# One-run operand for the up products, halved first block and last tile, spins, and bias rows spread in the first MLP

## The reference

```python
def first_block(x, ...):
    h = x
    for layer in range(DEPTH):              # 0: gated linear attention, 1: window attention
        h = h + mixer(rmsnorm(h, ln_mix[layer]))
        h = h + sq_relu_mlp(rmsnorm(h, ln_mlp[layer]), w_up[layer], w_down[layer])
    return rmsnorm(h, ln_final)

def second_block(x, p, ...):
    x = x + (gate_a * y_a + gate_b * y_b) @ w_out      # full and dilated attention
    x = x + jnp.square(jax.nn.relu(rmsnorm(x) @ w_ff1)) @ w_ff2
    gate_p = jax.nn.sigmoid(rmsnorm(x) @ w_ple_gate)
    x = x + gate_p * (p @ w_ple)
    return rmsnorm(x, final_norm_g)
```

## Time and profile before

| | us |
|---|---|
| median of 3 runs | 1064.34 (1063.89 to 1066.04) |
| the profiled execution | 1064.24 |
| its span, first to last instruction | 1062.4 |
| TensorE busy | 1012.1 |
| VectorE busy | 676.2 |
| ScalarE busy | 489.3 |
| GpSimd busy | 42.8 |

### The profile page before, as it was taken

The page is one execution under the profiler, slowest core; times in us unless marked ns, Lnnn a source line. Parts: engine busy times, 40 slices in busy tenths (PEclk is TensorE's granted clock), DMA queues, the critical chain, the costliest instruction groups (busy, mean ns, idle before and its releaser), DMA issues.

```text
span 1062.4 us, 12980 instructions
## 1 busy us (share of the span) xinstructions
PE 1012.1 (95%) x5384; PEld 849.5 (80%) x5384; DVE 676.2 (64%) x945; ACT 489.3 (46%) x573; POOL 42.8 (4%) x57
## 2 busy tenths in 40 slices
PE   6989999999999889999999999899999999999996
PEld 5866778888888767888888889877877788888875
DVE  4665766566656885754666656676656675466664
ACT  4353445344445653544444454334563454344452
POOL 1000100000000000000000013300000000000000
PEclk9989999999999999999999999999999999999999
DMA  7772376545564314765455555632335656545451
GB/s 214 249 262 80 119 238 224 173 160 197 199 214 143 120 50 149 250 217 197 159 188 180 201 183 161 196 100 80 99 109 178 195 175 215 188 159 197 180 175 43
DMA packets 115027, 180.99 MB, mean 170 GB/s; under 512 B 4351, under 2 KB 78567, under 8 KB 114968
## 3 DMA queue, kind: packets, MB, share of 16 engines
q1 hardware_dynamic: 114968, 180.16, 50.8%
HBM read 179.05 MB, written 5.55 MB: 174 GB/s over the span
## 4 chain that ended last, share of the span: by engine, by line
PE 85%; DVE 7%; ACT 2%; DMA 2%; POOL 2%; issue 1%; SPq 0%; DVEq 0%; POOLq 0%; ACTq 0%
PE ps L265 82%; PE ps L269 3%; DMA raw<-in_a_w_in 2%; DVE wlo L941 2%; DVE M L949 1%; DVE M L941 1%; POOL st L2186 1%; ACT M L1692 1%; ACT RR L1695 1%; ACT whi L1695 1%; POOL M L2186 0%; DVE M L945 0%; ACT M L1695 0%; DMA x<-in_x 0%; POOL st L2183 0%
## 5 line engine op out<-in xcount | busy, mean ns | idle before, releaser
L265 PE MATMUL ps<-whi,RR 128*128 128x512 f32 (+2 forms) x1568 | 494.6, 390 | 9.7 <-DVE wlo L941 6.0
L1695 ACT ACTIVATE whi<-raw 128x2048 fp32r<-128x2048 f32 (+1 forms) x161 | 302.3, 1881 | 196.6 <-PE ps L265 179.9
L941 DVE TENSOR_TENSOR wlo<-raw,whi 128x1024 fp32r<-128x1024 f32 (+1 forms) x322 | 372.5, 1200 | 29.9 <-ACT whi L1695 29.7
L265 PE MATMUL ps<-RR,whi 128*128 128x512 f32 (+1 forms) x1248 | 362.8, 357 | 10.9 <-DVE RR L949 5.6
L265 PEld LDWEIGHTS ps<-whi,RR 128*128 128x128 f32 x1568 | 293.9, 189 | 74.8 <-issue 9.6
L265 PE MATMUL ps<-wlo,RR 128*128 128x512 f32 (+2 forms) x784 | 303.2, 387 | 0.0
L265 PE MATMUL ps<-RR,wlo 128*128 128x256 f32 (+1 forms) x1008 | 284.5, 282 | 0.0
L265 PEld LDWEIGHTS ps<-RR,whi 128*128 128x128 f32 x1248 | 220.3, 190 | 50.6 <-issue 8.3
L265 PEld LDWEIGHTS ps<-RR,wlo 128*128 128x128 f32 (+1 forms) x1008 | 191.5, 190 | 0.9
L265 PEld LDWEIGHTS ps<-wlo,RR 128*128 128x128 f32 x784 | 148.4, 189 | 27.7
L941 DVE TENSOR_TENSOR M<-M,ps 128x512 f32<-128x512 f32 x56 | 38.5, 687 | 181.7 <-ACT M L1695 173.8
(11 more groups left out here) (88 smaller groups left out, 381.7 us busy)
## 6 DMA issues: line engine op xcount, KB each, us to landing
raw<-in_w_up SPq DMA_DIRECT2D x32, 1024.0 KB, 5.4
raw<-in_w_down SPq DMA_DIRECT2D x32, 1024.0 KB, 5.0
raw<-in_w_ff SPq DMA_DIRECT2D x32, 1024.0 KB, 5.3
raw<-in_w_in SPq DMA_DIRECT2D x23, 1024.0 KB, 5.1
raw<-in_a_w_in SPq DMA_DIRECT2D x12, 1024.0 KB, 7.1
raw<-in_a_w_out SPq DMA_DIRECT2D x4, 1024.0 KB, 5.0
raw<-in_b_w_q SPq DMA_DIRECT2D x4, 1024.0 KB, 5.3
raw<-in_b_w_out SPq DMA_DIRECT2D x4, 1024.0 KB, 5.0
```

The lines of the kernel that those rows point to most:

```text
L265: return pe.matmul(out, lhsT, rhs, start=start, stop=stop, skip_group_check=True)
L941: return dve.tensor_tensor(out, a, b, op)
L1695: return act.activation(out, in_, ACT.Copy, **k)
```

## The change

- `hT` and `hT2`: the high and the low part of a group k now lie side by side, so the up product's moving operand is one run of 512 columns, and the halves that others use are its two halves.
- Start: POOL writes the ones first. TensorE multiplies the ones by themselves, 128 columns, four times ahead of the gain's transpose and five times after it, into an unused bank. x and block 0 are loaded by halves in turn (x columns 0 to 511, rows 0 to 511 of the block, and the others). ACT and DVE split the first four groups of x, the first half of block 0, the other four groups, the second half. TensorE's first product goes by halves: groups 0 to 3 for both of its parts, then 4 to 7. The scale row (`rows_scale(0)`) comes after the second block instead of the first, and DVE evacuates both blocks then.
- The spreads of the bias rows: four DMAs each, one behind each of the loads up to block 18 (toe1) to 21 and 22 (toe2) to 25, and the bias of the first attention is read after block 29 instead of 20.
- End: the last product's last tile goes in two halves of 256 columns. The square is scaled inside ACT; POOL adds the sums one by one and takes the power. The gain is multiplied in before the power is known, into `SG`, and the last factor is left: ACT does it for rows 0 to 127, DVE for the others. The stores read `SG`.

```diff
@@ Views @@
-        self.hT, self.yT = parts(0), parts(4096)
-
-        self.hT2 = RR[:, 0:4096].rearrange("p (a k t) -> p k a t", a=2, t=T)
+        self.hT2 = RR[:, 0:4096].rearrange("p (k n) -> p k n", k=8)
+        self.hT, self.yT = (self.hT2[:, :, 0:T], self.hT2[:, :, T:2 * T]), parts(4096)
...
+LAST = [(0, 0, 512), (1, 0, 512), (0, 512, 1024), (1, 512, 768), (1, 768, 1024)]
@@ tensor_program: gemm_a, gemm_up, start, last product @@
-            for w_ in due(K.at("w_lo", j)):
-                pe.wait_ge(*w_)
...
-                        for w_ in due(ready(k)):
+                        for w_ in due(K.at("w_lo", (0, 0) if j == 0 and k < 4 else j), ready(k)):
...
-                        mm(b[:, i, :].rearrange("p (a t) -> p a t", a=2), hi[:, k, 128 * i:128 * i + 128],
-                           V.hT2[:, k, :, :], k == 0, False)
+                        mm(b[:, i, :], hi[:, k, 128 * i:128 * i + 128], V.hT2[:, k, :], k == 0, False)
...
+    def spin(n):
+
+        for w in due(K.at("ones")):
+            pe.wait_ge(*w)
+        for _ in range(n):
+            mm(K.banks[:, 3, 0:128], V.S["ones"][:, :], V.S["ones"][:, :], True, True)
+
+    spin(4)
     tile = ("g", 0)
...
     tr(b[:, 0:16], V.M[0:16, 0:128]).then_inc(*K.filled(tile))
+    spin(5)
     norm_rest(0)
...
-        if f == 0:
+        if f == 256:
             rows_scale(0)
...
-    g = gemm_a(("qk",), W, 0, 1024, hT, h_ready(0), None, after_qk)
+    g = gemm_a(("qk",), W, 0, 1024, hT, h_ready(0), lambda: None, after_qk)
...
-    run_all((gemm_b(("pg",), A["w_ple_gate_2"][0], 0, D, hT, h_ready(6)), 1))
+    ready = h_ready(6)
+    for f in (0, 512):
+        bs = acc_pair()
+        tiles = [(("pg", i), take(("pg", i), misc() if i == 4 else bs[LAST[i][0]])) + LAST[i]
+                 for i in range(5) if LAST[i][1] // 512 * 512 == f]
+        for k0 in (0, 4):
+            j, hi, lo = block(A["w_ple_gate_2"][0][k0 * 128:k0 * 128 + 512, f:f + 512], 4, 512)
+            for tile, b, c, n0, n1 in tiles:
+                for k in range(k0, k0 + 4):
...
+                    t = prod(b[:, 0:n1 - n0], hT[0][:, k, c * 128:c * 128 + 128], hT[1][:, k, c * 128:c * 128 + 128],
+                             hi[:, k - k0, n0 - f:n1 - f], lo[:, k - k0, n0 - f:n1 - f], k == 0, k == 7)
...
@@ vector_program @@
-    norm_rest(0)
-    lows_to(1)
+    def first_low(i):
+
+        h = slice(1024 * i, 1024 * i + 1024)
+        for w in due(K.at("w_hi", (0, 0) if i == 0 else 0)):
+            dve.wait_ge(*w)
+        tt(V.lo[:, 0, h], V.raw[:, 0, h], V.hi[:, 0, h].bitcast(F32), ALU.subtract).then_inc(
+            *K.up("w_lo", (0, 0) if i == 0 else 0))
+
+    norm_early(0)
+    first_low(0)
+    norm_turn(0, 2)
+    norm_turn(0, 3)
+    first_low(1)
+    block["lo"] = 1
     squares(0, *all_x(K, 0))
...
         if f == 0:
             diagonals(0)
+        if f == 256:
             rows_scale(0)
...
+        for f2 in {0: [], 256: [0, 256]}.get(f, [f]):
...
+    def gain(i):
+        c, n0, n1 = LAST[i]
+        for w in due(K.at("x_end", i), K.dma("fin")):
+            dve.wait_ge(*w)
+        tt(V.SG[:, c, n0:n1], x[:, c, n0:n1], M[:, n0:n1], ALU.mult).then_inc(*K.up("x_gain", i))
+
+    take()
+    take()
+    add(0)
+    add(1)
+    take()
+    gain(0)
+    gain(1)
+    take()
+    for i in (2, 3, 4):
+        add(i)
+    for i in (2, 3, 4):
+        gain(i)
+    for n in range(2):
+        s = V.SG[:, 1, 512 * n:512 * n + 512]
+        for w in due(K.at("rstd", ("end", 1)), K.at("x_gain", 4)):
+            dve.wait_ge(*w)
+        ts(s, s, st[:, 49:50], None, ALU.mult, None).then_inc(*K.up("y_end", (1, n)))
@@ scalar_program @@
-    norm_rest(0)
-    highs_to(1)
...
+    norm_early(0)
+    first_high(0)
+    norm_turn(0, 2)
+    norm_turn(0, 3)
+    first_high(1)
+    block["hi"] = 1
...
+        actf(V.PW[:, c, n0:n1], x[:, c, n0:n1], ACT.Square, scale=1.0 / 32, accum_out=st[:, 40 + i:41 + i]).then_inc(
+            *K.up("end_sq", i))
...
+    take()
+    take()
+    sig(2)
+    sig(3)
+    square(2)
+    sig(4)
+    square(3)
+    square(4)
+    for n in range(2):
+        s = V.SG[:, 0, 512 * n:512 * n + 512]
+        for w in due(K.at("rstd", ("end", 0)), K.at("x_gain", 2)):
+            act.wait_ge(*w)
+        copy(s, s, scale=st[:, 48:49]).then_inc(*K.up("y_first", (0, n)))
@@ pool_program @@
+    memset("ones", S["ones"][:, :], 1.0)
     memset("tab_end", S["tab"][32:33, :], -1e30)
     memset("half", S["half_"][:, :], -0.5)
-    memset("ones", S["ones"][:, :], 1.0)
...
@@ sync_program @@
         load("x%d" % n, 0, V.x[:, :, n * 512:n * 512 + 512], xd[:, :, n * 512:n * 512 + 512])
+        w = K.blocks[0][0][512 * n:512 * n + 512, :] if K.blocks else A["a_w_in"][0][0:512, 0:256]
+        load("w0" if n else "w_first", 0, V.raw[:, 0, 1024 * n:1024 * n + 1024].rearrange("p (k n) -> p k n", k=4),
+             w.rearrange("(k p) n -> p k n", p=128))
+    state["block"] = 1
     weights_to(4)
...
-    load("toe1", 0, A["toe1"], bass.AP(tensor=A["scr1"].tensor, offset=127, ap=[[383, 16], [-1, 128], [1, 256]]),
-         K.dma("scr1"))
-    load("toe2", 0, A["toe2"], bass.AP(tensor=A["scr2"].tensor, offset=127, ap=[[511, 12], [-1, 128], [1, 384]]),
-         K.dma("scr2", 2))
     weights_to(9)
...
-    weights_to(21)
-    load("bias", 0, V.BS, A["toe1"].rearrange("h p c -> p h c"), K.dma("toe1"), K.full(("to", 1, 1)))
+    for i in range(4):
+        weights_to(19 + i)
+        load("toe1", i, A["toe1"][4 * i:4 * i + 4], bass.AP(tensor=A["scr1"].tensor, offset=127 + 383 * 4 * i, ap=[
+            [383, 4], [-1, 128], [1, 256]]), K.dma("scr1"))
+    for i in range(4):
+        weights_to(23 + i)
+        load("toe2", i, A["toe2"][3 * i:3 * i + 3], bass.AP(tensor=A["scr2"].tensor, offset=127 + 511 * 3 * i, ap=[
+            [511, 3], [-1, 128], [1, 384]]), K.dma("scr2", 2))
+    weights_to(30)
+    load("bias", 0, V.BS, A["toe1"].rearrange("h p c -> p h c"), K.dma("toe1", 3), K.full(("to", 1, 1)))
...
-                 V.x[:, c, n * 512:n * 512 + 512], K.at("y_end", (c, n)))
+                 V.SG[:, c, n * 512:n * 512 + 512], K.at("y_end" if c else "y_first", (c, n)))
```

More of the change, by code:

```diff
@@ L925, in tensor_program @@
     run_all((g, 1))
-    run_all((gemm_b(("pg",), A["w_ple_gate_2"][0], 0, D, hT, h_ready(6)), 1))
+    ready = h_ready(6)
[7 more added lines that the diff above has]
+                for k in range(k0, k0 + 4):
+                    for w in due(K.at("w_lo", j), ready(k)):
+                        pe.wait_ge(*w)
+                    t = prod(b[:, 0:n1 - n0], hT[0][:, k, c * 128:c * 128 + 128], hT[1][:, k, c * 128:c * 128 + 128],
+                             hi[:, k - k0, n0 - f:n1 - f], lo[:, k - k0, n0 - f:n1 - f], k == 0, k == 7)
+                if k0:
+                    t.then_inc(*K.filled(tile))
+            if k0:
+                K.value["w_used", j] = K.full(tile)
+            else:
+                t.then_inc(*K.up("w_used", j))
 def vector_program(dve, K, V):
@@ L1153, in ev_qk @@
     def ev_qk(f):
-        tile = ("qk", f)
         if f == 0:
             diagonals(0)
+        if f == 256:
             rows_scale(0)
[L1158 to L1161, removed]
+        for f2 in {0: [], 256: [0, 256]}.get(f, [f]):
+            tile = ("qk", f2)
+            for w in due(K.full(tile), *rb(0)):
+                dve.wait_ge(*w)
+            stt(M[:, 2 * f2:2 * f2 + 512], K.bank(tile), 128 ** -0.5 if f2 < 512 else 1.0, RB[:, :], ALU.mult,
+                ALU.mult).then_inc(*K.emptied(tile))
         count["qk"] += 1
@@ L1669, in vector_program, with add @@
     run_all((g, 1))
-    run_all((gemm_b(1024, 8, ev_pg), 1))
-    for c in range(2):
-        for w in due(K.at("rstd", ("end", c)), K.dma("fin")):
+    def add(i):
+        c, n0, n1 = LAST[i]
+        s, xc, n = V.SG[:, c, n0:n1], x[:, c, n0:n1], n0 // 512
+        for w in due(K.empty(("pg", i)), K.empty(("pw", 512 * n, c))):
             dve.wait_ge(*w)
[L1674 to L1677, removed]
+        d = step(tt(s, s, V.PW[:, c, n0:n1], ALU.mult))
+        for w in due(d, K.full(("nt", 6, 3)), x_ready(K, 6, c, n)):
+            dve.wait_ge(*w)
+        tt(xc, xc, s, ALU.add).then_inc(*K.up("x_end", i))
+    def gain(i):
+        c, n0, n1 = LAST[i]
+        for w in due(K.at("x_end", i), K.dma("fin")):
+            dve.wait_ge(*w)
+        tt(V.SG[:, c, n0:n1], x[:, c, n0:n1], M[:, n0:n1], ALU.mult).then_inc(*K.up("x_gain", i))
[14 more added lines that the diff above has]
+        for w in due(K.at("rstd", ("end", 1)), K.at("x_gain", 4)):
+            dve.wait_ge(*w)
+        ts(s, s, st[:, 49:50], None, ALU.mult, None).then_inc(*K.up("y_end", (1, n)))
 def scalar_program(act, K, V):
@@ L1825, in mlp, with first_high @@
         norm_early(after)
-    norm_rest(0)
-    highs_to(1)
+    def first_high(i):
+        h = slice(1024 * i, 1024 * i + 1024)
+        for w in due(K.dma("w_first") if i == 0 else K.dma("w0", 0)):
+            act.wait_ge(*w)
```

(46 more changed lines are left out.)

8 lines of the change are left out of this document (removed).

## The result

The changed kernel takes 1075.08 us (median of 4 runs, 1074.95 to 1076.08), the kernel before 1065.19 in the same comparison; the ratio is 1.0096, with a 95% interval of 1.0078 to 1.0113. The forecast was 1047.9 us, its range ended at 1053.3. The profiled execution took 1074.95 us, its span is 1073.1.

The account below looks back on a forecast made before the run. TensorE, busy 95% of the span, was taken to bound the kernel, so edits pay by shortening its stream or a few waits. Gains 4.8 + 4.0 + 6.2 + 1.4 = 16.4 us; 1064.3 - 16.4 = 1047.9 us, range 1044.5 to 1053.3.

Parts of the forecast that it names:

- part three: Bias spreads moved into the first MLP: the stall near 60 us goes, 6.2 us gained, bounds 3.0 and 7.2.
- it needs about half of them: First MLP's weight queue: of the 5.4 us standing before the next load, a quarter spread needs about half, costed at nothing.
- Rival D: First MLP: the quarter spreads hold up the weights, slower if a quarter costs over 2.05 us; chance 0.03.
- D's last case: First MLP: all eight quarters hold TensorE by their whole 2.75 us, 22 us in all, 1069.9 us.
- B: Stall near 60 us: VectorE's gate chain takes its place, part three gives 3.0, time 1051.1 us; chance 0.14.
- Part one: Up products in all three MLPs: the moving operand in one run instead of two gains 4.8 us, bounds 0 and 9.9.
- A: Up products: the two runs cost nothing, part one gives 0, time 1052.7 us; chance 0.13.
- so the second run costs 6.2 ns: Up products: a pair takes 352.9 ns against 346.7 for plain ones, the difference laid on the operand's second run.
- Part two: Start: first product at 10.7 instead of 14.38 us, second block's end near 18.8; gain 4.0 us, range 1.9 to 5.0.
- C: Start: the high clock is there from 10.7 us, part two gives 5.0, time 1046.9 us; chance 0.12.
- Part four: End: halved last tile, POOL's scaling gone, gain multiplied ahead; net 1.4 us gained, bounds 0.8 and 1.9.
- E: Start and end: first product stays where it was, stores wait in line, both parts give 0, 1053.3 us; chance 0.03.

Follow-up runs that it names:

- P: The changed kernel with all eight bias-spread pieces cut by position instead of by heads, same bytes and queue places: 1055.02 us, ratio 0.9907 to the kernel before.

## Why the prediction was wrong

The step that failed is in part three: "One spread of 2,048 KB landed in 11.0 us, so a quarter is 2.75". A quarter of the bytes isn't a quarter of the time: the whole spread has 16 heads outermost, the quarter 4, and it moved at 95 GB/s, 5.5 us; a quarter of toe2 at 77 GB/s, 7.7 us. The Trainium skill says so (DMA: Bandwidth & Descriptors, Why a DMA increments its semaphore by 16 and not by 1): the number of engines is the largest up to 16 that divides the outermost dimension of both sides. The trace agrees for 4 and 8 heads (shares of 0.27 and 0.54); with 16 outermost the tail is gone, and with 12 a piece's packets start within 2.24 us, not 8.3. The next step fell with it, "it needs about half of them": by its own form, 5.4 + 7.7 - 6.66 = 6.4 us late for each tight load, not 1.5.

**Rival D** named the mechanism, the place and the point where the sign turns (2.05 us a piece). The loss was 20.3 us against P's MLP, 2.5 us a piece, near the 22 us that D's last case gave. But it didn't fall on eight pieces alike: TensorE waited four times, first at 175.85, when seven of the eight pieces had been issued, though the chain of waits holds late loads from 150.57 on. And 5.9 of some 20 us are the clock at half after the waits, which D didn't price. Its chance of 0.03 was the error of judgement: it stood on the 2.75.

**Part three** without that: the stall was worth 6.4 us by the medians and 4.8 by the spans (forecast 6.2, bounds 3.0 and 7.2). VectorE's low part, behind the gate chain, kept TensorE waiting for only 0.16 us at 58.91, so B falls.

**Part one**: 0 for 4.8; A was right (chance 0.13). The Trainium skill's rule (SBUF — State Buffer, Door 1: The DMA port swizzle) gives nothing for this edit, and the runs agree, at 1.0001. The step that failed is "so the second run costs 6.2 ns": both plain rows were of one size after the same size, and its own lower bound, "if the two sizes in turn are what costs", is the case.

**Part two**: 1.7 to 2.5 for 4.0. The steps held up to the second block (first product 10.80 for 10.7; VectorE done at 17.35 for 17.8), and 4.95 us were gained by then; what the sum left out, though the range allowed for it, is that the clock fell for 3.4 us at 31, 1.7 us. C falls: the products from 10.80 ran at half pace, until 14.2. The reason given against C doesn't carry, though: between the transposes of x and the products at 14.38 TensorE had been idle for 5.21 us. In the kernel without spins the transposes ended at 10.53 and the products began at 10.71, and the pace was full from 12.0.

**Part four**: 0.4 to 1.1 for 1.4. The stores' issue ended 1068.56 + 1.96 - 1065.41 = 5.1 us after the last matmul's start; before it was 1059.12 + 0.99 - 1053.38 = 6.7. That step held; of the sum of 1.4 the span shows 1.1.

E falls: the first product came 3.58 us earlier, and the stores didn't wait in line.

With the pieces cut by position the forecast would have been 1047.9 for a measured 1055.02: 4.8 of these 7 us are part one, the others mostly parts two and four.

## What to carry to other kernels

When a DMA is cut in pieces, cut an inner dimension and look at the outermost one of each piece: here 3, 4 and 8 heads outermost gave shares of 0.20, 0.27 and 0.54 of the engines, and slow pieces held up the loads behind them in their queue. Price a piece by a measured rate of the same outer shape, and take the price of an alternation from a row that alternates, before laying it on the operand's form. A load that comes late can cost more than its wait: here TensorE ran at half its clock after three of four waits.

## What the runs showed of the hardware

- **SP itself waits behind a piece**: issuing one weight load took 7.50 and 9.38 us behind pieces by heads, 0.37 us behind pieces by position. It isn't the cut by heads alone: in the kernel before, the first load behind the two whole spreads, at 40.08, took 9.39 us to issue. The queue looks full then; what limit this is, no run tells.
- **Pieces by heads on GpSimd's queue use more engines together**: busy share 0.72 with several in flight and nothing else moving, and 1.04 with weight loads beside them. The Trainium skill (the same section of DMA: Bandwidth & Descriptors) says that on this queue such a DMA takes its few engines in turn from a moving start; the 0.72 agrees, the engines themselves aren't in the profile.
- **The turn from 512 to 256 columns**: 236 ns for the 512-column product when a 256-column one follows each time, 230 in runs of eight; the 256-column one takes 117 and 119, so a pair loses 4 ns of 353.
- **Clock falls of 3.4 us**, 1.7 us each, come in some profiled executions and not in others of nearly the same kernel: near 31 us in P but not in the kernel with the old end, whose start is the same; near 680 to 700 in ten of the twelve; at 83, 94, 350 and 360 in one each. One between 372 and 393 us is in all twelve. They are as large as parts two and four.
